# One inference step of a gated hybrid encoder layer: RMS factors applied to x in the first phase, evacuations without factors, units and norms in another order

## The reference

```
xn = rmsnorm(x) * norm_g
h  = xn @ w_in       # columns qa ka va ua qi ki wi qb kb vb ub ga gb
A: scores = sum_h wi_h * relu(qi_h . ki);  mask = top-k of the scores
   A = softmax(rope(rmsnorm(qa)) . rope(rmsnorm(ka)) / 8 + mask) @ va
B: z = qb . kb / 8;  a = sigmoid(z) * prod of sigmoid(-z) over later keys;  B = a @ vb
y  = x + (sigmoid(ga) * ((A * silu(ua)) @ w_a) + sigmoid(gb) * ((B * silu(ub)) @ w_b)) @ w_o
```

## Time and profile before

| | us |
|---|---|
| median of 3 runs (lowest, highest) | 575.59 (575.29, 576.33) |
| the profiled execution's own time | 571.5 |
| its span, first to last instruction | 569.7 |
| PE busy | 535.4 (94%) |
| DVE / ACT / POOL busy | 335.7 / 224.0 / 88.4 |
| mean granted TensorE clock | 0.988 |

### The profile page before, as it was taken

The page is one execution under the profiler, slowest core; times in us unless marked ns, Lnnn a source line. Parts: engine busy times, 40 slices in busy tenths (PEclk is TensorE's granted clock), DMA queues, the critical chain, the costliest instruction groups (busy, mean ns, idle before and its releaser), DMA issues.

```text
span 569.7 us, 10250 instructions
## 1 busy us (share of the span) xinstructions
PE 535.4 (94%) x4344; PEld 506.1 (89%) x4344; DVE 335.7 (59%) x663; ACT 224.0 (39%) x354; POOL 88.4 (16%) x89
## 2 busy tenths in 40 slices
PE   6999998699999979998998799999999999999998
PEld 5889898599999969997997688898899999999997
DVE  5905669999997875983283456663245433456331
ACT  6623664311445365454324366643413323123110
POOL 3413000210132266324440000000000000000000
PEclk9999999999999999999899799999999999999999
DMA  8620202334220210017122005021033212227311
GB/s 326 216 112 26 85 1 75 117 132 169 74 76 1 76 55 21 1 65 267 44 74 75 2 1 186 16 75 39 1 112 110 75 62 88 75 95 279 139 49 50
DMA packets 15358, 50.45 MB, mean 89 GB/s; under 512 B 2416, under 2 KB 5872, under 8 KB 11728
## 3 DMA queue, kind: packets, MB, share of 16 engines
q1 hardware_dynamic: 15168, 49.79, 24.3%
q10 hardware_dynamic: 144, 0.00, 0.0%
HBM read 42.82 MB, written 6.82 MB: 87 GB/s over the span
## 4 chain that ended last, share of the span: by engine, by line
PE 80%; DVE 11%; ACT 6%; issue 2%; DMA 1%; DVEq 0%; ACTq 0%
PE PS L529 31%; PE PS L746 13%; PE PS L807 9%; PE PS L789 6%; PE PS L483 3%; PE PS L660 3%; DVE wlo L1130 3%; PE PS L639 3%; PE PS L515 3%; ACT whi L853 2%; PE PS L615 2%; DVE bias L1304 1%; DVE bias L1265 1%; PE PS L724 1%; DVE top L1263 1%
## 5 line engine op out<-in xcount | busy, mean ns | idle before, releaser
L529 PE MATMUL PS<-xhi,whi 128*128 128x272 f32 x320 | 95.7, 299 | 8.4 <-DVE oT L1235 3.4
L1130 DVE TENSOR_TENSOR wlo<-raw,whi 128x2048 fp32r<-128x2048 f32 (+1 forms) x36 | 76.8, 2135 | 34.4 <-ACT whi L853 34.4
L529 PE MATMUL PS<-xlo,whi 128*128 128x272 f32 x320 | 93.7, 293 | 0.0
L529 PE MATMUL PS<-xhi,wlo 128*128 128x272 f32 x320 | 93.4, 292 | 0.0
L853 ACT ACTIVATE whi<-raw 128x2048 fp32r<-128x2048 f32 (+1 forms) x36 | 61.7, 1717 | 73.1 <-PE PS L746 33.9
L529 PE MATMUL PS<-whi,xhi 128*128 128x256 f32 x256 | 75.4, 295 | 6.0 <-ACT vals L902 6.0
L529 PE MATMUL PS<-wlo,xhi 128*128 128x256 f32 x256 | 73.3, 286 | 0.0
L529 PE MATMUL PS<-whi,xlo 128*128 128x256 f32 x256 | 72.8, 284 | 0.0
L529 PEld LDWEIGHTS PS<-xhi,whi 128*128 128x128 f32 x320 | 61.6, 192 | 12.5 <-issue 5.2
L529 PEld LDWEIGHTS PS<-xhi,wlo 128*128 128x128 f32 x320 | 61.7, 193 | 0.0
L529 PEld LDWEIGHTS PS<-xlo,whi 128*128 128x128 f32 x320 | 61.5, 192 | 0.0
(11 more groups left out here) (217 smaller groups left out, 1162.6 us busy)
## 6 DMA issues: line engine op xcount, KB each, us to landing
raw<-in_w_units SPq DMA_DIRECT2D x28, 1024.0 KB, 5.0
raw<-in_w_mixes SPq DMA_DIRECT2D x8, 512.0 KB, 3.5
stage<-in_x_kw_qi SPq DMA_DIRECT2D x7, 564.0 KB, 8.7
res<-in_x_kw_qi SPq DMA_DIRECT2D x1, 2176.0 KB, 8.0
out<-res SPq DMA_DIRECT2D x16, 136.0 KB, 1.7
out<-vals SPq DMA_DIRECT2D x2, 1024.0 KB, 6.5
out<-kT SPq DMA_DIRECT2D x1, 1088.0 KB, 4.6
out<-tm SPq DMA_DIRECT2D x1, 1024.0 KB, 4.9
```

Source lines behind the costliest of these rows:

```text
L529: mm = pe.matmul(out, lhsT, rhs, start=(k == 0), stop=(k == 23))
L1130: dve.tensor_tensor(wlo[:, uu % 2, 0:n], raw[:, uu % 2, 0:n], whi[:, uu % 2, 0:n].bitcast(F32), ALU.subtract).then_inc(w_lo, 1)
```

## The change

- **First phase.** x is scaled in place. After the two first `w_low`, DVE adds xhi and xlo back into `xs` (over the staging area), and after the RMS factor is there it multiplies xs by rB; ACT and DVE split it again into xhi and xlo, chunk by chunk, when PE has done with the chunk (`chunk_done`). POOL makes the sample's copy `xst` again. The sums of squares go to PE behind chunk 3, rB behind chunks 4 and 5. ki, wi and qi are still made from unscaled x.
- **Evacuations.** No factors are left in them. kb and qb move from DVE to ACT; for u, ACT takes the sigmoid straight from PSUM, DVE multiplies it with PSUM, and POOL's product is gone. Gates 2 to 7 get their sigmoid on ACT straight from PSUM, DVE's pass is gone.
- **Order.** Another order of units, one more unit ahead of branch B, `POST_B` of 5 groups in place of 11. K's norms go into `PRE_B`, Q's into branch B from slot 16 on, with two buffers of squares. Indexer products have 4 banks in place of 6, fill groups have 4 banks there. `topk(3)` runs 4 times among the products instead of 12.
- **Tables and loads.** Two small activations ask for the tables of Exp and Sigmoid ahead of use, the split of gate0 moves behind the first exp of branch A, and SP's loads follow the new order.

```diff
-UNITS = [(n, KIND[n[:2]]) for n in ("vb0", "vb1", "kb1", "ub0", "kb0", "qb0", "qb1", "ka0", "ka1", "ub1", "qa0", "qa1",
+UNITS = [(n, KIND[n[:2]]) for n in ("vb0", "vb1", "ka0", "ka1", "kb0", "kb1", "qb0", "qb1", "ub0", "qa0", "qa1", "ub1",
...
-DOT_FILL = groups_of("vb1")[4:] + groups_of("kb1") + groups_of("ub0")[:3]
+DOT_FILL = groups_of("vb1")[4:] + groups_of("ka0") + groups_of("ka1")[:2]
-PRE_B = groups_of("ub0")[3:] + groups_of("kb0", "qb0")
+PRE_B = groups_of("ka1")[2:] + groups_of("kb0", "kb1", "qb0")
-B_FILL = groups_of("qb1", "ka0", "ka1", "ub1", "qa0", "qa1", "ua0")[:B_SLOTS]
-POST_B = groups_of("ua0")[2:] + groups_of("ua1", "va0")
+B_FILL = groups_of("qb1", "ub0", "qa0", "qa1", "ub1", "ua0", "ua1")[:B_SLOTS]
+POST_B = groups_of("va0")
-K_SLOT, Q_SLOT = 11, 25
+K_SQUARE, K_SCALE = 3, 10
+Q_SQUARE, Q_ROTATE = 16, 22
...
+                if c == 3:
+                    pe.wait_ge(x_added, KC)
...
+                if c == 4:
+                    pe.wait_ge(r_wide_ready, 1)
+                    for t in range(4):
+                        last = pe.matmul(ps[:, 5, P * t:P * t + P], r_wide[:, t, :], ident, start=True, stop=True)
+                    last.then_inc(rb_done, 1)
...
+            for c in range(KC):
+                last = dve.tensor_tensor(xs[:, c, :], xhi[:, c, :].bitcast(F32), xlo[:, c, :].bitcast(F32), ALU.add)
+            last.then_inc(x_whole, 1)
             dve.wait_ge(x_ss, 1)
...
+            def scaled(c):
+                dve.tensor_tensor(xs[:, c, 0:SEQ], xs[:, c, 0:SEQ], rB[:, 0:SEQ], ALU.mult).then_inc(xs_scaled, 1)
+            def normed_low(c):
+                dve.wait_ge(xn_hi, c + 1)
+                dve.tensor_tensor(xlo[:, c, 0:SEQ], xs[:, c, 0:SEQ], xhi[:, c, 0:SEQ].bitcast(F32),
+                                  ALU.subtract).then_inc(xn_lo, 1)
...
+            def normed_high(c):
+                act.wait_ge(xs_scaled, c + 1)
+                if c < KC - 1:
+                    act.wait_ge(chunk_done, c + 1)
+                else:
+                    act.wait_ge(qi_done, 5)
+                act.activation(xhi[:, c, 0:SEQ], xs[:, c, 0:SEQ], ACT.Copy).then_inc(xn_hi, 1)
...
-                act.activation(silu_tmp, su[:, 2 * int(name[2]) + f, halved(h)], ACT.Sigmoid).then_inc(u_sig, 1)
+                act.activation(silu_tmp, ps[:, BANK[g], 0:HALF_NT], ACT.Sigmoid).then_inc(u_sig, 1)
...
+                    dve.wait_ge(u_sig, U_GROUPS.index(g) + 1)
+                    ins = dve.tensor_tensor(su[:, 2 * int(name[2]) + f, halved(h)], bank, silu_tmp, ALU.mult)
...
-                if b != 3 and n % 2:
+                if b in (1, "s") and n % DOTS_PER_FILL == DOTS_PER_FILL - 1:
                     topk(3)
```

More of the change, by code:

```diff
@@ L407, in _ @@
             load_unit("qb1")
[L408 to L413, removed]
+            load_unit("ub0")
+            load_unit("qa0")
+            group_out_wait(sp, LAST_GROUP[U["kb1"]])
             sp.dma_start(new_b_k_fm, kT[:, :, 0:NT]).then_inc(st_kb, 16)
-            for name in ("ka1", "ub1", "qa0", "qa1", "ua0"):
-                load_unit(name)
+            load_unit("qa1")
+            load_unit("ub1")
             sp.wait_ge(k_rows, 1)
@@ L542, in _ @@
             last.then_inc(kw_tr, 1)
[L543 to L550, removed]
+            for g in groups_of("vb0"):
                 group(g)
@@ L704, in _ @@
                 item(n)
[L705 removed]
+            for g in POST_B[2:]:
                 group(g)
@@ L901, in evacuate @@
                     act.wait_ge(st_ki, 32)
-                ins = act.activation(dst, bank[0:n, 0:UC], ACT.Copy, scale=xrs[0:n, t:t + 1])
+                ins = act.activation(dst, bank[0:n, 0:UC], ACT.Copy)
                 if t == 4:
@@ L964, in _, with square_tile @@
                     filled(DOT_FILL[n // DOTS_PER_FILL])
-            for g in PRE_B:
+            def square_tile(t, c, k, name):
+                n = TILES[t][1]
+                group_out_wait(act, FIRST_GROUP[U[name]] + t)
+                if t == 4:
+                    act.wait_ge(sample_rows, sample_units(name))
+                if k >= 2:
+                    act.wait_ge(summed_up, k - 1)
+                act.activation(squares[k % 2][0:n, :], tm[0:n, t, c:c + W], ACT.Square).then_inc(squared, 1)
+            for k, g in enumerate(PRE_B):
                 filled(g)
+                if K_SQUARE <= k < K_SQUARE + 5:
+                    square_tile(k - K_SQUARE, W, k - K_SQUARE, "ka1")
             def sigmoids(t):
@@ L1014, in _ @@
                 filled(mine[1])
-                squares(2 * t + 1)
-            for g in POST_B[:2]:
-                filled(g)
+                query_squares(2 * t + 1)
             def item(n):
@@ L1034, in item @@
                 ins.then_inc(item_out, 1)
+            filled(POST_B[0])
             for n in K_ITEMS:
                 item(n)
-            for g in POST_B[2:-2]:
-                filled(g)
+            filled(POST_B[1])
             for n in Q_ITEMS:
                 item(n)
-            for g in POST_B[-2:]:
+            act.activation(esum[:, 0:2], unity, ACT.Exp)
+            for g in POST_B[2:-1]:
                 filled(g)
+            evacuate(POST_B[-1])
             def exps(t):
@@ L1074, in _ @@
                     exps(t)
+                if t == N_STEPS:
+                    act.activation(top[:, 0, 0:2], unity, ACT.Sigmoid)
                 if 1 <= t <= N_STEPS:
```

336 lines of the change are left out of this document (176 added, 160 removed).

## The result

| | before | changed |
|---|---|---|
| median of 4 runs of each on one chip (lowest, highest) | 575.44 (575.14, 576.33) | 555.03 (554.48, 557.93) |
| the profiled execution's own time, its span | 571.5, 569.7 | 554.89, 553.1 |
| PE / DVE / ACT / POOL busy | 535.4 / 335.7 / 224.0 / 88.4 | 530.0 / 328.7 / 229.5 / 76.1 |
| mean granted TensorE clock | 0.988 | 0.994 |

The ratio is 0.9653, with a 95% interval of 0.9618 to 0.9688: faster, by 3.5%. Forecast were 560 us, in a range of 552 to 570. In a later comparison (e10) the same two kernels stood at 574.00 and 558.64, ratio 0.9731 (0.9691 to 0.9772); the experiments say why. Two slow executions are left out of the ratios: the profiled one of e9 (671.95 us, from 509 us on at a granted clock of 0.16 with PE busy throughout) and one of the kernel before beside e5 to e8 (2907 us).

A forecast was written before the change was run, and what follows sets the result against it. The prediction took PE as the bound, busy 535.4 of 569.7 us. Its terms, 8.8 + 0.3 - 8.5 - 2.1 - 6.4 - 6.5 - 0.9 = -15.3, took 571.5 to 556.2; the 4.1 profile-to-median difference gave 560, range 552 to 570.

The forecast's parts named there:

- First phase, +8.8: Before chunk 5, PE waits 6.8 us for the widened factors and loses 2.0 to the lower clock: 8.8 us slower.
- the index rows: Ahead of the index products, a new PE wait of 1.6 less a vals wait of 1.3 that goes: +0.3.
- the first wait is not there: Rival: the first-phase wait is absent or too short for the clock to fall, 555 us; chance 0.08.
- Products, -8.5: Index products and top-8: DVE falls to 30 us, under PE's 32; idle 7.3 and clock 1.7 go, 0.5 returns.
- Branch B, -2.1: In branch B the 3.1 us wait goes and 1.0 is counted for late DVE: 2.1 us faster.
- the rival by which DVE bounds B: DVE, at 108 of 119 us, makes PE wait in branch B: 584 us if 3.1 in all eight steps; chance 0.12.
- Between the branches, -6.4: Between branches B and A, waits of 2.9 and 1.8 and 1.7 of clock go: 6.4 us faster.
- Start of branch A, -6.5: At branch A's start, waits of 4.0 and 0.6 and 2.4 of slow group go, 0.5 returns: 6.5 us faster.
- L746, -0.9: Loading the Sigmoid table ahead of the end takes away L746's wait: 0.9 us faster.
- the gates, 0: In the mix stage, 416 to 512 us, DVE's gate pass goes and ACT's becomes two: no change.
- From 556.2 to 560: Whole kernel: the 4.1 us between profiled execution and median of the kernel before was added to the profile-based 556.2.
- The exclusive lock: Part of the DVE-bound rival: DVE passes meeting POOL on shared ports in branch B, 117 of 119 us, 571; chance 0.05.

The follow-up runs named there:

- e10: The changed kernel run again, unaltered, on the same chip as the later experiments: 558.64 us, 0.9731 of the kernel before.
- e9: e6 with ACT evacuating the first group of vb1 ahead of the index transposes' copies: 541.77 us, 0.9447 of the kernel before.
- e5: Changed kernel with means behind vb0's low half, DVE waiting for POOL's wide factors before its additions, vb1's low half behind the last xlo: 550.44 us.
- e8: Changed kernel with a single buffer for the squares of ka and qa in place of two: 562.90 us.
- e1: Changed kernel with DVE's means right behind vb0's low half, ahead of vb1's low half and the eight additions: 553.50 us.
- e4: Changed kernel with topk(3) run 12 times among the index products again in place of 4: 562.16 us.
- e12: Changed kernel with Q's factors, gains and rotation six slots later: 561.22 us.
- e3: Changed kernel with DVE's low half of gate0 moved from behind step 0 to behind step 1 of branch A: 553.50 us.
- e11: Changed kernel with branch A's old start: gate0's split and low half ahead of the first masks and exp, small Exp gone: 559.62 us.
- e6: e5 and e3 together, plus two PE moves: first vb1 group ahead of index transposes, gate2's last half group behind branch A's last product: 543.42 us.

## Why the prediction was right, point by point

- **First phase, +8.8 (with the index rows +9.1): right, measured +9.3.** The wait at L525 was forecast as 6.8 and is 6.7; the additions end at 32.4. The clock was put at 2.0: the matmuls of rB and chunk 5 take 6.45 in the changed kernel and 4.53 in e1, so 1.9. The new wait at the index rows is 1.7, forecast 1.6. e5 shows that the wait was DVE's order of work, together with POOL's exclusion beside it, and could be avoided. It was worth 8.1 us there; the prediction's rival "the first wait is not there" put only 5 on it.
- **Products, -8.5: right, as far as tried.** DVE fell to 23.4 of 32 us, further than the 30 forecast. e4 gives 4.1 back for the rounds. The 0.5 for four banks did not come: there is no wait.
- **Branch B, -2.1: too careful by 1.0.** DVE was forecast at 108 of 119 and has 99.4 of 124. Its lateness costs PE nothing, and the rival by which DVE bounds B did not come. e8 confirms the cause of the wait that went, and shows its mechanism.
- **Between the branches, -6.4: right.** e12 gives back 3.6 of wait and 2.4 of clock in its profile. Cover was enough, since the rotation is done at 277, 13 us ahead of PE's transposes.
- The three together are -20.0 and not -17.0. Idle time fell by 15.4 (16.9 to 1.5), where the steps counted 13.6: the 1.5 allowed for banks and B, and some small waits. The remaining 1.2 are slow stretches of before beyond the 3.4 counted.
- **Start of branch A, -6.5: the direction was right, one term was mis-sized.** "0.5 comes back where the low half of gate0 now stands ahead of the second masks": 2.76 came. The low half (2.29) was counted as if the second masks had slack. e3 takes 2.2 away by moving it. e11's 3.8 of wait and 2.3 of slow matmuls are the size that the rest of the step was given. That the stretch to the end still fell by 6.0 is luck of that one profile: behind the 2.76 no slow matmuls came, where e10's profile loses 4.2 behind the same two waits. And the sum of -15.3 against -16.6 is so near because this shortfall and the 3.0 gained in the middle work against each other.
- **L746, -0.9, and the gates, 0: right.** The wait is not among the waits after, and PE is busy for all of 400 to 500 us.
- **From 556.2 to 560: wrong as a step, and harmless by chance.** The profiled executions give 571.5 to 554.89, which is near the 556.2. The 4.1 between a profile and the median was carried over as a constant, but in the first comparison it was 3.9 for the kernel before and 0.1 for the changed one, in e10's comparison the changed kernel's profile lay 1.6 above its median. For the changed kernel that is largely the changing price of waits in clock (e10); for the kernel before the cause stays open, since its times and its clock go together less closely (571.54 us at 0.982, 573.92 at 0.985). The medians fell by 20.4 in one comparison and by 15.4 in the other; the steps' 15.3 lies at the lower end.
- **The exclusive lock was given 0.05, as a way for B to be late.** That rival did not come, but the lock has its cost: low halves of 3.9 in place of 2.2 in B, and up to 3.9 us on a power of 1.0 in e1. In the changed kernel both fall where nobody waits.

## What to carry to other kernels

When a step is moved into a phase, put the part that another engine waits for ahead of the bulk of the work, and leave the other engine's path free: in these traces a small instruction of POOL did not finish until 0.9 us behind the last of a row of long two-input ones of DVE. Count for each wait of PE that stays a second price, the matmuls at the lower clock behind it, which one profile may show and the next not; take out the last small waits together, since then the spread went as well (from 6.8 us to 0.4 on the same chip). And when a piece of work is moved behind "the first" of a pair of steps, price the second step as its next victim.

## What the runs showed of the hardware

- POOL's 128x4 power took 1.0 us with DVE idle, 3.0 beside one DVE instruction of 2.2 and 4.9 beside four in a row, in both ending 0.9 behind the last of them; in the other direction a DVE subtraction of 2.2 took 3.9 behind the start of a POOL product of 2.0.
- A wait of PE of only 1.1 us was followed by matmuls at the lower clock in some executions (48 in 7.79 us) and not in others (6.26). The waits of 1.7 at L589 and 1.1 at L834 were followed by it in neither profile of the changed kernel. With no wait in the middle of the kernel longer than 1.6 us, no execution of e6 or e9 in their ratios showed a clock below 0.999.
- A load of ACT's function table cost 1.28 us on the path, with the next activation 0.01 behind it.
